# One subtraction in place of four for the low half of each weight chunk, in a float32 transformer kernel

## The reference, cut to what matters

```python
def first_block(x, c, ctx, c_ctx, ...):
    for i in range(DEPTH):                                   # A, then B
        shift, scale, gate = jnp.split(jax.nn.silu(c) @ ada_w + ada_b, 3, axis=-1)
        h = modulate(x, g_norm, shift[:, None], scale[:, None])      # rmsnorm(x, g) * (1 + scale) + shift
        hc = modulate(ctx, g_norm, shift_c, scale_c)
        if i % N_MIXERS == 0:
            y, yc = mixer_a(h, hc, *mp, cos_a, sin_a, not last)
        else:
            y, yc = mixer_b(h, hc, *mp, cos_b, sin_b, not last)
        x = x + gate[:, None] * y
    return rmsnorm(x, final_g)

def mixer_a(h, hc, w_in, sinks, w_o, cos, sin, ctx_out):
    q, k, v, g = jnp.split(h @ w_in, [...], axis=-1)
    ...                                                      # rope, scores, softmax, o = p @ v
    return (o * jax.nn.silu(g)) @ w_o

def hybrid_mixer(h, w_in, b_in, conv_w, conv_b, rpb, ml_norm_w, w_out):
    proj = h @ w_in + b_in
    na_out = neighbourhood_attention(na_q, na_k, na_v, rpb) * jax.nn.silu(na_z)
    ...                                                      # short convolution, recurrent memory
    return jnp.concatenate([na_out, ml_out], axis=-1) @ w_out
```

## Time and profile before

| | |
|---|---|
| median of 3 executions | 1178.09 us (1177.7 to 1179.01) |
| the profiled execution | 1179.01 us, its span 1177.2 us |
| mean granted TensorE clock | 0.989 |
| PE busy | 1106.4 us, 94% of the span |
| DVE busy | 721.3 us, 61% |
| ACT busy | 651.9 us, 55% |
| POOL busy | 416.7 us, 35% |
| L2509 on POOL | 396 instructions, 300.0 us |

### The profile page before, as it was taken

The page is one execution under the profiler, slowest core; times in us unless marked ns, Lnnn a source line. Parts: engine busy times, 40 slices in busy tenths (PEclk is TensorE's granted clock), DMA queues, the critical chain, the costliest instruction groups (busy, mean ns, idle before and its releaser), DMA issues.

```text
span 1177.2 us, 20182 instructions
## 1 busy us (share of the span) xinstructions
PE 1106.4 (94%) x7408; PEld 903.1 (77%) x7408; DVE 721.3 (61%) x1582; ACT 651.9 (55%) x1363; POOL 416.7 (35%) x512
## 2 busy tenths in 40 slices
PE   4899999999998799999899999999999999999896
PEld 0588778877886689877677878798878778887685
DVE  6365666676668526263877878645767774526545
ACT  4614455555556526642766768746567653447633
POOL 1633112202120334674300002316654326446871
PEclk9999999999999999999999999999999999999898
DMA  9741333422112221132222121042212405213112
GB/s 354 266 144 59 138 141 139 149 108 99 46 28 90 74 72 37 54 123 75 57 88 66 29 82 46 7 157 81 77 48 74 148 19 144 73 54 126 38 35 72
DMA packets 34253, 109.33 MB, mean 93 GB/s; under 512 B 4516, under 2 KB 7076, under 8 KB 33772
## 3 DMA queue, kind: packets, MB, share of 16 engines
q1 hardware_dynamic: 34156, 108.05, 27.6%
HBM read 101.39 MB, written 2.11 MB: 88 GB/s over the span
## 4 chain that ended last, share of the span: by engine, by line
PE 76%; DVE 9%; ACT 4%; POOL 4%; issue 3%; DMA 2%; SPq 1%; DVEq 0%; POOLq 0%; ACTq 0%
PE PS L673 32%; PE PS L656 14%; PE PS L789 8%; PE PS L777 7%; PE PS L968 6%; PE PS L1032 3%; DMA AF<-wstream 2%; POOL AR L2509 2%; PE PS L873 1%; PE PS L708 1%; ACT AF L1255 1%; DVE AF L1956 1%; DVE AF L2035 1%; DVE AD L2331 1%; PE PS L1007 1%
## 5 line engine op out<-in xcount | busy, mean ns | idle before, releaser
L2509 POOL TENSOR_TENSOR AR<-AF,AR 128x256 fp32r<-128x256 f32 x396 | 300.0, 790 | 605.8 <-ACT AR L1132 605.7
L673 PE MATMUL PS<-AR 128*128 128x512 f32 (+1 forms) x2208 | 454.9, 363 | 11.9 <-POOL AR L2509 4.1
L673 PEld LDWEIGHTS PS<-AR 128*128 128x128 f32 x2208 | 367.6, 191 | 79.3 <-issue 18.5
L656 PE MATMUL PS<-AR 128*128 128x256 f32 (+4 forms) x1284 | 245.9, 328 | 7.9 <-ACT AF L1255 3.3
L656 PEld LDWEIGHTS PS<-AR 128*128 128x128 f32 (+1 forms) x1284 | 181.1, 191 | 43.0 <-issue 22.0
L1264 ACT ACTIVATE AF<-PS 128x512 f32<-128x512 f32 (+3 forms) x192 | 124.3, 648 | 109.6 <-PE PS L777 105.5
L1255 ACT ACTIVATE AF<-PS,AF 128x512 f32<-128x512 f32 (+3 forms) x192 | 140.7, 733 | 22.2 <-DVE AF L2308 13.2
L777 PE MATMUL PS<-AF 128*128 128x128 f32 x864 | 128.1, 275 | 10.0 <-DVE AF L1956 6.7
L777 PEld LDWEIGHTS PS<-AF 128*128 128x128 f32 x864 | 100.2, 140 | 34.9 <-issue 15.2
L1132 ACT ACTIVATE AR<-AF 128x1024 fp32r<-128x1024 f32 x99 | 103.4, 1052 | 42.1 <-PE PS L968 27.9
L789 PE MATMUL PS<-AF 128*64 128x128 f32 x1728 | 115.7, 279 | 2.1 <-DVE AF L1963 2.1
(11 more groups left out here) (212 smaller groups left out, 1129.6 us busy)
## 6 DMA issues: line engine op xcount, KB each, us to landing
AF<-wstream SPq DMA_DIRECT2D x171, 512.0 KB, 4.6
AF<-x_in SPq DMA_DIRECT2D x2, 1024.0 KB, 8.6
AD<-rows SPq DMA_DIRECT2D x4, 512.0 KB, 5.8
out<-AF SPq DMA_DIRECT2D x16, 128.0 KB, 1.9
AF<-AF SPq DMA_DIRECT2D x28, 64.0 KB, 2.0
AF<-rpb_band SPq DMA_DIRECT2D x8, 224.0 KB, 4.6
BIAS<-rpb_band SPq DMA_DIRECT2D x8, 224.0 KB, 4.7
AF<-ctx_in SPq DMA_DIRECT2D x1, 1024.0 KB, 5.3
```

The lines of the kernel that those rows point to most:

```text
L656: mm = pe.matmul(out, stationary, moving, start=i == 0, stop=i == len(products) - 1)
L673: mm = pe.matmul(out[:, 0:t1 - t0], a, b, start=k == 0 and i == 0, stop=k == nk - 1 and i == 2)
L2509: ins = pool.tensor_tensor(w[:, 1, at:at + 256], raw(c)[:, at:at + 256], w[:, 0, at:at + 256].bitcast(F32), ALU.subtract)
```

## The change

In `feed`, the low half of a weight chunk is written by one subtraction of 128x1024 elements. Before, a loop did it in four, of 128x256 each, of which the last counted up `lo_done`. Now the one instruction does. The wait for `hi_done` ahead of it, the place of the call among POOL's other work and all else are as they were: on each engine the instructions stand in the same order as before, only that each four of L2509 are one.

```diff
@@ -2505,10 +2505,8 @@
                     c = chunk_at[name]
                     pool.wait_ge(hi_done, fed[0] + 1)
                     w = weight(name)
-                    for at in range(0, CHUNK, 256):
-                        ins = pool.tensor_tensor(w[:, 1, at:at + 256], raw(c)[:, at:at + 256],
-                                                 w[:, 0, at:at + 256].bitcast(F32), ALU.subtract)
-                    ins.then_inc(lo_done, 1)
+                    pool.tensor_tensor(w[:, 1, :], raw(c), w[:, 0, :].bitcast(F32),
+                                       ALU.subtract).then_inc(lo_done, 1)
                     fed[0] += 1
```

## The result

The changed kernel takes 1189.07 us (median of 4; 1188.93 to 1190.34) against 1177.89 (1176.81 to 1179.01) before: ratio 1.0097, 95% interval 1.0086 to 1.0109, or 11.4 us slower. I had forecast 2.8 us slower, with a range up to 1184.5. The sign was right and the size wrong, and the range didn't hold the time.

What follows compares the result with a forecast made beforehand. It took PE, busy 94% of the span, as the bound, with POOL mattering only where PE waits for it. Losses of 5.95 less gains of 3.1 made +2.8 us: 1180.9 from the median 1178.09, range 1175.5 to 1184.5.

Steps and rivals of the forecast that it cites:

- The new operation: On POOL, one 1024-column subtraction takes 2.38 us against 2.81 for four pieces, 0.43 saved per chunk, 43 us in all.
- The gains: Places where PE waits for POOL's work, directly or through other operations, get shorter: 3.1 us saved in sum.
- The three waits for a chunk: PE's three waits for L2509, 4.1 us together, shrink by 1.15 us in all.
- the late queue: Near the end, PE's waits for L2618 and L2637 stand behind two chunks: 0.86 us gained once.
- the 0.4 at 48.61: In the first 60 us, the chunk directly ahead of an activation's low half ends earlier: 0.4 us gained.
- The holds that were named: DVE operations held by the undivided POOL instruction at 382, 388, 542, 815, 970 and near 98 us: 5.95 us lost.
- A's end: End of A's attention, 382 and 388 us: L2015 held beside two chunks, costing PE 1.5 and 1.1 us.
- the two small ones: L1893 at 542 us and L1924 near 98 us, held beside chunks: 0.8 us lost together, between 0 and 3.4.
- The cover in C's attention: Elsewhere in attention, DVE keeps PE one to several us ahead of need, so held operations cost nothing.
- more places than I count: Rival: two further holds of 1.5 us reach PE, 3 us more, giving 1183.9 us; chance 0.10.
- A sign of the prediction: PE's waits for L1956 rise from 6.7 to 10 us or more; no growth despite long DVE operations refutes the forecast.
- The start: The pair of chunks at 24.93 us, freeing weight-stream buffers, changes nothing: 0 taken, between -0.9 and +1 us.

Runs made afterwards that it cites:

- the 16 chunks: Kernel before, with the undivided subtraction only at 16 chunks where PE waits for POOL, four pieces at the other 83: ratio 0.9991, -1.1 us.
- the 79: Kernel before, with 79 chunks undivided and four pieces kept at the 20 where a held VectorE operation reached PE: ratio 0.9994, -0.7 us.
- the part alone: Kernel before, with the undivided subtraction only for the 12 chunks of C's attention (867 to 972 us): ratio 1.0051, +6.0 us.
- the second execution: Second profiled execution of the changed kernel, all 99 chunks undivided, from its repeat timing: span 9.0 us longer than the kernel before.
- the second timing: The changed kernel, all 99 chunks undivided, timed once more against the kernel before: ratio 1.0107, +12.6 us.
- four groups: Four runs on the kernel before, undivided only at: first three chunks, +1.1 us; A's end, +2.7; C's attention, +6.0; chunks 6, 43, 55, +2.0.

## Why the prediction was wrong, by its own steps

- **The new operation: right.** 2.38 us where nothing disturbs it, as worked out from 768 and 256 columns. POOL's chunk time fell by 59 us, not 43, because a record's length includes POOL's own waits: before, the 300.0 us are 22 more than 99 x 2.81, and after, the 240.8 are 5 more than 99 x 2.38.
- **The gains: too large.** The three waits for a chunk gave 1.6 (taken: 1.15), the wait at 574.83 fell from 1.07 to 0.66 as forecast, and the late queue gave 0.8 (0.86). L2597's 0.3 came to 0.2 and was lost with 0.6 more in a wait for ACT. For the 0.4 at 48.61 no run shows anything: the wait of 0.38 behind it is gone in the changed kernel, but PE came there over 4 us late. Together some 2.2 us in the traces; in the medians the 16 chunks that hold all of it come to -1.1 (-2.0 to 0) and the 79 to -0.7 (-2.7 to +1.2). The 3.1 lie outside both.
- **The holds that were named: right, each a little small.** A's end 3.0 in gaps (2.6 forecast), 970: 1.5 (1.4), 815: 1.6 (1.15), the two small ones 0.9 (0.8). L2015 lasted 2.60 (2.6 forecast), L2167 2.27 (2.2) and L1956 2.48 (2.2).
- **The cover in C's attention: the step that failed.** "Elsewhere in attention a held DVE operation has PE one to several us ahead of need, so I count it at nothing": DVE was 0.3 us ahead of PE's need at 912 and not ahead at all at 942. I had looked at waits for L1956, and in the stretches of A and B; in C, the operation held is L2210, which PE doesn't wait for directly, and each hold is handed on through L2232, L1963 and ACT until PE meets it. It cost 0.7 + 1.9 + 1.3 = 3.9 us, and the part alone +6.0 with 970 and the clock. The rival "more places than I count" had this mechanism and three quarters of its price (3 us), at 0.10. The cover wasn't wrong everywhere: ten other held operations cost PE nothing.
- **A sign of the prediction that misled.** It said that it would be wrong if PE's waits for L1956 didn't grow. Their total fell, from 6.7 to 6.3, while the holds were there: the lateness came out under other names (L1963, L2015, L2167), and two of the old waits shrank because PE was late. The total by name was the wrong place to look.
- **The start: taken at 0, with +1 as the end.** Alone it came to +1.1 (-0.6 to 2.7). In the changed kernel's two profiled executions PE was 2.7 and 1.0 us late at 40 us.
- **The clock: no term at all.** Behind a hold of 2 us or so the matmuls often ran at the lower clock, but not each time: in the 15 us behind A's end in two of three profiled executions with undivided chunks there (0.89 and 0.77, and 1.00), in the 15 us behind C's end in three of the four with chunks in one or two pieces there (0.89 each, and 1.00) and in none of the ten others. It cost 1.1 us at each of the two ends in the first execution of the changed kernel and nothing in the second. The profiled executions of other variants had low stretches at other places (near 50, 330 and 1110 us), before as well, and matmul by matmul that is where executions of like kernels part; I take it for most of the scatter of 3 us around a median, which no run isolates.

Of the forecast's 2.8 us to the 9.0 of the second execution, where the ends have no low clock: C's attention 3.9, the start 1.0, gains that didn't come 0.9, and 1.0 for named holds that were larger. They sum to 6.8, where 6.2 is to be explained. From there to the measured 11.4, and 12.6 at the second timing, the rest stays open. The clock is my guess for it: the mean granted clock of 29 executions of the changed kernel is 0.9850 and that of 84 of the kernel before 0.9864, by which, as an estimate, 0.0014 x 1180 = 1.7 us of PE's full speed are missing. The cause of the main loss is shown by the parts: 20 of the 99 chunks, undivided in four groups, give +11.8 us together, and the other 79 no loss that can be told from none.

## What to carry to other kernels

The length of a single GpSimd instruction is a cost to VectorE even where GpSimd is idle two thirds of the time: four instructions made into one save 0.4 us a chunk on one engine and hold the other's operations by some 2 us (2.60 against 0.42). Look for every VectorE operation with two SBUF inputs near the long instruction (and for those with one, as L1956 was held too), also those that nobody waits for directly, and follow the lateness to the end before calling it covered. An instruction that ends sooner also moves the next one, which can then be the one that holds (L2597 beside L2335). Two traces whose matmuls come in the same order, laid beside each other, show all of this where totals of waits hide it; and one profiled execution of each isn't enough to price the clock. A width chosen by place (long where the matmul engine waits for the result, short beside VectorE's critical work) beat either width used throughout.

## What the runs showed of the hardware

- A VectorE operation of 8 columns took 2.26 us because a 1024-column GpSimd subtraction was in its way; one of 256 columns 2.60 instead of 0.42. The whole instruction counts, not the columns of the one that waits. By this rule (the Trainium skill, "SBUF — State Buffer", "Who interferes with whom": the pair of ports is held for the whole instruction, and the other engine is blocked, not slowed) the forecast's losses counted in full, and the trace agrees at the five largest of the named places, where the operations lasted 2.27 to 2.60 us.
- An operation with one of its operands in PSUM wasn't held: L2232 kept its 0.76 us beside the 1024-column chunk of 919.83 us.
- Two VectorE operations in a row took turns with two GpSimd ones: 3.90 us for the pair beside two halves, 3.92 beside one whole, 2.81 beside four quarters. The second and third of the quarters waited in turn (a chunk of 4.51 instead of 2.81).
- Doubling GpSimd's busy time in short instructions left the pair at 2.89.
- A 128-column piece takes 0.46 us by its record, where an eighth of the 1024-column one's 2.38 would be 0.30; undisturbed, a chunk in eight pieces is some 1 us longer than one undivided, and used everywhere this was nearly as slow as the undivided form (1.0088 against 1.0107).
